# How many retention heads run ahead of the output product: four instead of seven

## The reference

```python
proj = x @ w_in                      # 2048 -> 3*1024 + 4*1024 columns
sb  = stick_breaking_attention(sb_q, sb_k, sb_v)      # 8 heads of 128
sb  = sb * rsqrt(mean(sb*sb) + eps) * sb_norm_w
ret = retention(rotary(r_q), rotary(r_k), r_v)        # 8 heads of 128
ret = (ret - mu) * rsqrt(var + eps) * ret_norm_w      # per head and token
ret = silu(r_g) * ret
mixed = concatenate([sb, ret])
x = layer_norm(ALPHA * x + mixed @ w_out)
# then peer_ffn(x) and a second layer_norm
```

## Time and profile before

| | |
|---|---|
| Median of 3 executions | 2268.61 us (2268.48 to 2272.78) |
| The profiled execution | 2266.69 us, its span 2264.9 us |
| TensorE (PE) busy | 2104.1 us, 93% of the span |
| VectorE (DVE) busy | 1631.0 us, 72% |
| ScalarE (ACT) busy | 1108.1 us, 49% |
| Mean granted TensorE clock | 0.976 of full |

### The profile page before, as it was taken

How to read it: one execution, slowest core, us unless ns; L and a number is a source line. 1 busy time by engine, 2 the same in 40 slices (tenths; PEclk the granted TensorE clock), 3 DMA queues, 4 the chain that set the end, 5 groups by cost and what they waited for, 6 DMA issues and landing times.

```text
span 2264.9 us, 42561 instructions
## 1 busy us (share of the span) xinstructions
PE 2104.1 (93%) x12326; PEld 1860.0 (82%) x12326; DVE 1631.0 (72%) x2645; ACT 1108.1 (49%) x1888; POOL 270.6 (12%) x171
## 2 busy tenths in 40 slices
PE   8998898979878778889999999999999999999995
PEld 7887786768777777879999999998788888888884
DVE  4556656665588888989999999996555555555556
ACT  4554454445422222334666666655455555555552
POOL 0003301000100000002444444410000000000001
PEclk9999998989999999999999999999999999999998
DMA  7764452647444444545555555566865565555552
GB/s 231 221 207 144 142 169 82 209 144 205 135 125 119 122 112 124 144 139 164 161 157 158 159 157 157 159 174 200 225 202 191 193 193 194 193 192 192 193 194 103
DMA packets 253812, 378.42 MB, mean 167 GB/s; under 512 B 41809, under 2 KB 173009, under 8 KB 253137
## 3 DMA queue, kind: packets, MB, share of 16 engines
q1 hardware_dynamic: 253776, 377.98, 55.7%
HBM read 373.69 MB, written 4.19 MB: 167 GB/s over the span
## 4 chain that ended last, share of the span: by engine, by line
PE 51%; DVE 13%; issue 7%; DVEq 1%; SPq 0%; DMA 0%; ACT 0%; POOL 0%; ACTq 0%
PE ps L406 16%; PE ps L407 16%; PE ps L408 16%; DVE split_lo L1229 5%; PE ps L650 3%; DVE ps L1240 1%; DVE onehot L1397 0%; DVE onehot L1392 0%; DVE head_i L1299 0%; DVE pick_n L1402 0%; SPq L383 0%; DMA raw<-in_expert_v 0%; DVE head_p L1319 0%; DVE head_i L1307 0%; DVE head_p L1316 0%
## 5 line engine op out<-in xcount | busy, mean ns | idle before, releaser
L972 DVE TENSOR_TENSOR split_lo<-raw,split_hi 128x512 fp32r<-128x512 f32 x864 | 623.6, 725 | 519.6 <-ACT split_hi L717 519.4
L717 ACT ACTIVATE split_hi<-raw 128x512 fp32r<-128x512 f32 x864 | 544.4, 631 | 605.8 <-PE ps L408 588.7
L406 PE MATMUL ps<-act_hi,split_hi 128*128 128x256 f32 x2048 | 607.9, 297 | 82.5 <-DVE split_lo L1229 81.6
L407 PE MATMUL ps<-act_lo,split_hi 128*128 128x256 f32 x2048 | 586.5, 286 | 0.0
L408 PE MATMUL ps<-act_hi,split_lo 128*128 128x256 f32 x2048 | 586.0, 286 | 0.0
L876 ACT ACTIVATE split_hi<-ps 128x512 fp32r<-128x512 f32 x512 | 292.6, 594 | 465.3 <-DVE ps L1240 252.6
L406 PEld LDWEIGHTS ps<-act_hi,split_hi 128*128 128x128 f32 x2048 | 399.3, 195 | 107.2 <-DVE split_lo L1229 105.7
L406 PE MATMUL ps<-split_hi,whalf_hi 128*128 128x512 f32 x1024 | 398.7, 389 | 3.2 <-DVE split_lo L972 3.2
L407 PEld LDWEIGHTS ps<-act_lo,split_hi 128*128 128x128 f32 x2048 | 400.6, 196 | 0.0
L408 PEld LDWEIGHTS ps<-act_hi,split_lo 128*128 128x128 f32 x2048 | 399.5, 195 | 0.0
L407 PE MATMUL ps<-split_lo,whalf_hi 128*128 128x512 f32 x1024 | 398.4, 389 | 0.0
(11 more groups left out here) (172 smaller groups left out, 1448.8 us busy)
## 6 DMA issues: line engine op xcount, KB each, us to landing
raw<-in_expert_u SPq DMA_DIRECT2D x1024, 128.0 KB, 2.9
raw<-in_expert_v SPq DMA_DIRECT2D x256, 512.0 KB, 4.6
raw<-in_w_in SPq DMA_DIRECT2D x112, 512.0 KB, 3.8
raw<-in_w_out SPq DMA_DIRECT2D x32, 512.0 KB, 4.1
raw<-in_w_pq SPq DMA_DIRECT2D x128, 128.0 KB, 2.8
cst<-in_tables SPq DMA_DIRECT2D x4, 576.0 KB, 5.1
x_nat<-in_x SPq DMA_DIRECT2D x4, 512.0 KB, 6.9
x_dram<-x_cols SPq DMA_DIRECT2D x1, 2048.0 KB, 7.9
```

Of the source, the lines that this page charges most:

```text
L406: nc.tensor.matmul(acc, l_hi, r_hi, start=first, stop=False)
L407: nc.tensor.matmul(acc, l_hi, r_lo, start=False, stop=False)
L717: nc.scalar.activation(split_hi[:, q % SPLITS, :], raw[:, q // 2, q % 2, :], ACT.Copy).then_inc(hi_ready, 1)
L972: vec.tensor_tensor(split_lo[:, q % SPLITS, :], raw[:, q // 2, q % 2, :], split_hi[:, q % SPLITS, :].bitcast(f32), ALU.subtract).then_inc( ...
```

## The change

```diff
-RT_FIRST = 7
+RT_FIRST = 4
```

## The result

The changed kernel takes 2275.69 us (median of 13 executions, 2273.37 to 2280.53), the kernel before 2271.99 us in 13 executions (2267.45 to 2277.31). The ratio is 1.0019 with a 95% interval of 1.0010 to 1.0028, that is 2.3 to 6.4 us more. The forecast was +4.8 us and 2273.4. The median of before was 2268.61 us from 3 executions when the forecast was made; over 13 it is 3.4 us higher, so the forecast is best compared by its difference.

A forecast was written before the change was run, and what follows sets the result against it. TensorE and VectorE were taken as almost level, VectorE's normalisation releasing the second join. Restart 4.6 us later plus 0.2 for the clock gave +4.8: 2268.6 to 2273.4 us, own range 2271.9 to 2275.1, with rivals 2270.0 to 2276.5.

The forecast's parts named there:

- What bounds the stretch: Product stage: TensorE and VectorE almost level; VectorE's normalisation of the retention heads, without any room, releases the second join.
- The front: Ahead of the product: three heads leave, the turn starts between 381.1 and 381.7, tile 0 gains 4.3 us.
- The loop: Between product tiles: three more heads cost TensorE 5.3 us, plus 0.5 for new waits, bounds 0 to 1.2.
- the rival of the spared clock: Joins and first product tiles: clock stays full from 381 us, no fall; +2.0 us, 2270.6; chance 0.18.
- VectorE's chain: Head 7's statistics to last gate product: L1095 ends at 409.0, first norm step 412.0, last gate product 422.7 instead of 417.89.
- The second join: Last turn's start to second half's first tile: 2.8 us, was 2.99; restart at 425.5, 4.6 us later.
- Behind it: After the second join: 0.2 us more for the clock, up to 0.9 possible; the shift goes to the end.
- The heads didn't hide: Rival, product loop: three heads and their waits fit under the product, 5.8 us less; -1.0 us, 2267.6; chance 0.03.
- The longer low clock: Rival, both joins: low from the turn through most of the first four tiles, and longer after second join; 2275.4; chance 0.13.
- Slower by over 0.2%: Whole kernel: time beyond the 4.5 us that can be told from no change, over 2273.1; chance 0.50.
- the forecast's own range: Whole kernel: 3.3 to 6.5 us more, 2271.9 to 2275.1, from tile 0's start, waits and clock.
- the wide one: Whole kernel: range taking in the rivals on both sides, 2270.0 to 2276.5 us.

The follow-up runs named there:

- the second pair of profiles: The changed kernel and the kernel before, each profiled once more without an edit: layer norm's turn 146.07 and 141.05 us after L754, 5.02 apart.
- `early7`: Against the kernel before, seven heads ahead as there, with statistics, power and normalisation in two parts, heads 0 to 3 first: ratio 0.9978 (0.9967 to 0.9988).
- `es7`: Against the kernel before, seven heads ahead, norm steps in two parts and the two ln1 loads spread among the w_out loads: ratio 0.9966 (0.9952 to 0.9979).
- `busy4`: The changed kernel plus 24 unused transposes between the second join's two turns, keeping TensorE busy: ratio to the kernel before 1.0021 (1.0011 to 1.0032).

## Why the prediction was right, and where its steps were not

*What bounds the stretch.* Right. The chain that sets the second join is head 7's statistics, the variances, GpSimd, ten norm steps on a full VectorE, the last gate product. Shown from both sides: the trace after has each link within 0.6 us of the forecast, and taking the norm steps of heads 0 to 3 off the chain behind head 7 gives 3.8 us back.

*The front.* 3.8 us were gained at tile 0, where I took 4.3. The low clock ran through the transposes and they took 3.40 us instead of 1.94, as I had thought likelier; the turn itself started 0.2 later than the nearest end of my estimate.

*The loop.* The sum was near (+5.39 against +5.8), and that was luck: its terms were not right. Three heads are 5.28. I had added 0.5 for waits and left the loss of 1.7 us to the clock where it was. After, the loop takes 420.48 - 389.61 = 30.87 us; less 16 x 1.36 and 4 x 1.76 this leaves 2.07 for waits, while the windows show full clock from tile 0 on. So the waits were mis-sized: 2.1 instead of 0.8 with head 7's own, over the upper bound of 1.5 too. About 0.2 of them is tile 13, which started late for its split; the sum had that split just in time. The clock gave 1.7 back at the same time and hid it. The rival of the spared clock was thus half true: the fall was spared in the loop, but the clock was low in both turns. Two of the other waits, ahead of head 4's z product and of its values, in the timeline after:

```profile
393.13 0.30 PEld L506 LDWEIGHTS ps<-qk_t 128*128 128x128 f32 x2 [0.47 <-issue]
...
395.88 0.30 PEld L515 LDWEIGHTS ps<-proj,soft_a 128*128 128x128 f32 x2 [0.43 <-DVE soft_a L1045]
```

*VectorE's chain.* L1095 0.6 us earlier than the sum had it, GpSimd's power 3.35 instead of 2.90, the norm steps 425.55 - 414.75 = 10.8 as against 10.7. The end of the last gate product was missed by 0.1, though it hangs on the loop: the waits that the sum lacked and the low clock that it had too much cancel in it as well.

*The second join.* 428.98 - 425.60 = 3.4 us from the turn to the first tile, where I took 2.8: the low clock made the turn 1.97, and VectorE waited for ScalarE between the fills. This term is 0.6 too small, and nothing offsets it: with 0.1 less from the last gate product it is the miss of 0.5 at the second half's start.

*Behind it.* I took 0.2 more for the clock; the second pair of profiles has -0.1. That the shift goes through to the layer norm is shown there (5.15 at the join, 5.02 at the layer norm's turn). From that turn to the end of the span, the four profiles of the two kernels took 1762.9 and 1763.7 us with four heads, 1763.1 and 1765.9 with seven, so nothing that the change does shows there.

*The rivals.* The heads didn't hide. The longer low clock came true in the two turns (3.40 and 1.97 us) and not in the tiles behind them: from the second half's first matmul to its fifth tile are 7.1 us, 7.2 before. Slower by over 0.2% had 0.50, within had 0.46; at 1.0019 with this interval the measurement itself doesn't decide between the two.

*The numbers.* The difference was right: 4.8 forecast, 4.3 by the ratio and 5.0 by the second pair of profiles. In absolute time 2275.69 us lies past the upper end of the forecast's own range (2275.1) and within the wide one (2276.5) only, because the median of before, from 3 executions, was 3.4 us low. The lower end of the forecast's own range is a slip: 1.2, 0.5 and 0.2 off 4.8 leave 2.9 and not 3.3.

Open stay two points: why the same gap lets the clock fall in one kernel and not in another, and why the norm steps in two parts shorten a wait in the search far behind them. The 3 to 4 us by which the ratios of `early7` and `es7` lie below what their profiles show up to the layer norm's turn are mostly the 3.0 us behind it, of which 1.9 are that wait.

## What to carry to other kernels

Before moving work from one stage into the next, follow the longest chain that hangs on the moved work across the engines, and not only the engine that is busiest: here TensorE lost 1.6 us and VectorE's normalisation, which could only start after the last head, 4.7. A reduction over many heads should be split, so that what is ready is normalised in the gaps and only the last part stands at the join. And a gain at one join is only a gain once the loads behind it are early enough; look for the next stand before counting it. A ratio says how much, not where: two marks, one ahead of the edit and one behind it, show whether the gain was made where the edit is.

## What the runs showed of the hardware

One fall of the granted clock cost about 1.7 us (the loop of before), a third of what the change costs, and the length of the gap ahead of it doesn't decide alone. Ahead of tile 0 TensorE stood 1.90 us in the kernel before and the clock fell afterwards; with six heads it stood 1.89 us and the clock stayed at full. At the second join it fell behind a wait of 0.93, a turn of eight transposes and a wait of 1.91, and it stayed up behind sixteen transposes in one piece and a wait of 2.09 (`early7`), though at the first join of the same kernel it fell (0.55) behind sixteen transposes and a wait of 1.90. What the prediction took from the Trainium skill (TensorE: Matmul & The Clock Gate, HAM oscillation), that a gap throttles and is paid again at every gap, is not borne out for waits of about 2 us; the page says it of a kernel with longer waits, for a DMA. On transposes, the Trainium skill (TensorE: Matmul & The Clock Gate, Part 4: PE-mode transpose) has them not counted as work in the same way. These float32 transposes don't agree: with 24 of them in the wait of `busy4`, the turn of 8 behind them ran at full clock (1.09 us), where without the 24 it ran at half (1.97 us).

A load of 512 KB was so late behind two broadcasts of 1024 KB on the same queue that TensorE stood for 0.7 to 4.3 us; in the four kernels that issue the two between the tiles, with `sub_keys` still ahead of them all, it did not stand. In the listing of DMA issues, 400 to 470 us of the profile after (KB each, median us to landing), the broadcasts take over twice as long as the tiles:

```profile
raw<-in_w_out SPq DMA_DIRECT2D x18, 512.0 KB, 4.2
ln_w<-in_ln_w SPq DMA_DIRECT2D x1, 1024.0 KB, 11.1
ln_b<-in_ln_b SPq DMA_DIRECT2D x1, 1024.0 KB, 9.8
```

And one profile is one execution: two profiles of the changed kernel differed by 3.6 us at one stand and the clock behind it, most of what the change is worth. Counted from a mark that the change can't move, the two profiles of each kernel agree to a few hundredths of a us up to the second half's first matmul, and no further.
